# First block's output product as three fp32r products, one eighth of it inside the recurrence

## The chip, the cores and the metric
The kernel runs on one core of a Trainium2 chip. The metric is device time in microseconds, median of three runs. The engines are TensorE (PE, with its weight loads as PEld), VectorE (DVE), ScalarE (ACT), GpSimd (POOL) and SyncE (SP), which issues most loads. All waits between them are semaphores that the kernel sets itself.

## The reference
Two transformer blocks of 256 tokens, width 1024, all in fp32. The change lies in the first one:

```python
x = x + FFN_HALF * swiglu(rms_norm(x, norm_ffn1), ffn1_gate, ffn1_up, ffn1_down)
p = rms_norm(x, norm_mix) @ w_in
o_sb = stick_breaking_attention(q, k, v)      # 8 heads of 64, then rms_norm per head
o_rw = rwkv7_time_mix(rw_in, ...)             # 8 heads of 64, a recurrence in chunks of 64 tokens
x = x + jnp.concatenate([o_sb, o_rw], axis=-1) @ w_out          # 1024 x 1024: the changed product
x = x + FFN_HALF * swiglu(rms_norm(x, norm_ffn2), ffn2_gate, ffn2_up, ffn2_down)

# recurrence: S_t = S_{t-1} diag(w_t) + (S_{t-1} a_t) b_t^T + v_t k_t^T ;  y_t = S_t r_t
# end of rwkv7_time_mix, per head:
yn = (y - mean) * lax.rsqrt(var + LNX_EPS) * ln_w + ln_b
return (yn + bonus) * g
```

## The kernel before
**Data.** Activations between products lie transposed, features on the 128 partitions and 256 tokens along the row. SBUF is cut by hand: `ring` holds six weight slots of 2048 columns, `arena` 27 blocks of 1024 columns (`A(j)`, `tiles(j)`; `AR(j)` is the same memory as fp32r). PSUM is `ps`, eight banks of 512. A weight matrix streams through the ring; the load of item n waits until item n - 6 is used (`w_used`).

**Precision.** Most products are done as three fp32r products (`mm3`, L824): an operand is split into a rounded high part and the rest, and high*high, low*high and high*low are summed. For weights ScalarE makes the high part (L1612) and VectorE subtracts the rest in the ring slot (`split`, L2179). The output product used plain fp32 instead: one `mm` (L774), which the trace shows as two records.

**Order.** Each engine runs its own list; nothing is scheduled at run time. The recurrence is a loop over four chunks. In each, TensorE makes the right side, ScalarE copies it (`rhs_kept`), TensorE multiplies by the inverse (`rec_u`), VectorE copies that (`u_kept`), TensorE adds it to the state and to y, VectorE scales the state (L2478 to L2480), ScalarE copies y (`y_kept`). Beside it VectorE finishes one quarter of the attention half per chunk (`sb_out`, L2464 and L2465). After the last chunk:

1. TensorE takes head means (`y_mean`), VectorE centres y, ScalarE squares it, TensorE takes variances (`y_var`), ScalarE the root (`y_root`), VectorE the reciprocal (L2499), the product (L2500) and the sum (L2501), which is the recurrent half of the mix (`rw_out`).
2. The output product is `out_rows(N_WOUT, c)` for c = 0 to 3: 128 x 512 products, two feature tiles f by two token tiles t by two halves h, so 8 per c and 32 in all, summed in banks 4 to 7. c = 0 and 1 need the attention half, c = 2 and 3 the recurrent half. c = 0 stands in two halves around the variances.
3. Then the next feed-forward begins: ScalarE and VectorE split its first three weight tiles, VectorE adds the product to x (`add_rows`, L2205), ScalarE squares the rows and takes roots, VectorE scales (L2173), TensorE transposes (`turn_apart`, L795).

On VectorE the three splits stand between `rw_out` and `add_rows`:

```python
tt(mix[1], y_n, bonus, ALU.add).then_inc(S("rw_out"), 1)
for n in range(HI_RING):
    split(N_FFN2 + n)
add_rows("x2_done", N_WOUT + 4, 1.0)
norm_rows("n3")
```

## Time and profile before

| | |
|---|---|
| time of three runs | 1105.42 us median (1105.32 to 1107.82) |
| the profiled execution's own time | 1107.49 us |
| its span, first to last instruction | 1105.7 us |
| TensorE busy, weight loads | 98%, 81% |
| VectorE, ScalarE, GpSimd busy | 61%, 41%, 3% |
| chain that ended last | TensorE 89%, VectorE 6%, ScalarE 3% |
| mean granted clock of TensorE | 0.997 of 2.4 GHz; digit 9 in all 40 slices |

The profile gives each instruction's start and length. "Idle before" is the time in which the engine waited, with the instruction that released it. The chain is followed back from the last instruction. Ends of matmuls are modelled and overlap, so the distance of two starts is a better measure of a matmul than its length. "Busy" for TensorE means that some matmul was in flight, not that it ran at its best. All times of the rows are from the span's start; the changed part lies at 340 to 397 us.

### The profile page before, as it was taken

The page shows a single profiled execution, that of the slowest core. Times are in us where ns is not written, and L with a number is a line of the kernel's source. Part 1 is how long each engine was busy: PE and PEld are TensorE (multiplying, and loading weights), DVE is VectorE, ACT ScalarE, POOL GpSimd, SP SyncE. Part 2 cuts the span into 40 slices and gives each one's busy share as a digit, 9 for nine tenths or more (in the row PEclk, how much of TensorE's full clock was granted, in tenths as well). Part 3 has the DMA queues.
Part 4 walks back from the last instruction along what each step waited for, and adds up shares of the span by engine and source line. Part 5 has one row for each costly group of instructions (what it writes and reads, how often), then busy time and mean ns, then how long its engine had stood idle before and what let it go on. Part 6 is the DMA issues. An engine that isn't in the chain of part 4 may idle for free.

```text
span 1105.7 us, 19149 instructions
## 1 busy us (share of the span) xinstructions
PE 1086.0 (98%) x8232; PEld 892.5 (81%) x8232; DVE 672.0 (61%) x848; ACT 448.1 (41%) x573; POOL 35.3 (3%) x30
## 2 busy tenths in 40 slices
PE   9999999999999999999999999999999999999997
PEld 8999999999988479999988999988999753434343
DVE  6488777789564856778766573277559542222123
ACT  6333334764542254333325242467583521211112
POOL 0000000000340000000003000000000000000000
PEclk9999999999999999999999999999999999999999
DMA  9976756454300349689862353332357979999994
GB/s 333 391 264 227 255 183 202 142 155 151 116 3 2 114 158 332 233 287 333 306 218 76 114 193 113 115 115 83 109 195 298 373 316 408 421 410 418 421 419 198
DMA packets 121012, 254.29 MB, mean 230 GB/s; under 512 B 6241, under 2 KB 91505, under 8 KB 109426
## 3 DMA queue, kind: packets, MB, share of 16 engines
q1 hardware_dynamic: 119890, 250.54, 62.1%
q10 hardware_dynamic: 1056, 2.79, 0.8%
q8 instruction: 51, 0.84, 0.3%
q14 instruction: 15, 0.12, 0.0%
HBM read 252.25 MB, written 1.06 MB: 229 GB/s over the span
## 4 chain that ended last, share of the span: by engine, by line
PE 89%; DVE 6%; ACT 3%; issue 1%; DMA 0%; SPq 0%; ACTq 0%; DVEq 0%
PE ps L827 54%; PE ps L774 33%; ACT arena L1612 2%; DVE ring_r L2179 1%; ACT arena_r L1612 1%; DVE ring_r L2312 1%; PE ps L1357 1%; DVE arena L2499 1%; DVE arena L2366 1%; DMA x<-in_x 0%; DVE arena L2381 0%; PE ps L795 0%; ACT gb_r L1612 0%; PE ps L1562 0%; PE ps L783 0%
## 5 line engine op out<-in xcount | busy, mean ns | idle before, releaser
L827 PE MATMUL ps<-hall_r,arena_r 128*128 128x256 f32 x1632 | 299.6, 281 | 0.0
L827 PE MATMUL ps<-arena_r 128*128 128x256 f32 (+1 forms) x1216 | 286.3, 325 | 0.0
L2179 DVE TENSOR_TENSOR ring_r<-ring,arena_r 128x2048 fp32r<-128x2048 f32 x88 | 203.1, 2312 | 109.4 <-ACT arena_r L1612 106.9
L827 PEld LDWEIGHTS ps<-hall_r,arena_r 128*128 128x128 f32 x1632 | 252.8, 188 | 1.2 <-issue 0.3
L1612 ACT ACTIVATE arena_r<-ring 128x2048 fp32r<-128x2048 f32 (+1 forms) x101 | 191.1, 1899 | 150.1 <-PE ps L827 139.8
L827 PE MATMUL ps<-hall_r,ring_r 128*128 128x256 f32 x816 | 227.8, 279 | 0.0
L827 PEld LDWEIGHTS ps<-arena_r 128*128 128x128 f32 x1216 | 203.9, 189 | 18.9 <-issue 0.7
L1612 ACT ACTIVATE arena<-ps 128x512 f32<-128x512 f32 (+3 forms) x136 | 80.4, 605 | 302.2 <-PE ps L827 188.0
L774 PE MATMUL ps<-arena 64*64 64x32 f32 (+7 forms) x1944 | 188.6, 321 | 4.1 <-ACT arena L1612 1.3
L774 PEld LDWEIGHTS ps<-arena 128*64 128x64 f32 (+3 forms) x1944 | 110.7, 143 | 64.8 <-issue 57.0
L827 PEld LDWEIGHTS ps<-hall_r,ring_r 128*128 128x128 f32 x816 | 154.9, 190 | 0.9
L827 PE MATMUL ps<-arena_r,ring_r 128*128 128x256 f32 (+1 forms) x432 | 123.4, 286 | 0.0
L827 PE MATMUL ps<-ring_r,arena_r 128*128 128x512 f32 (+1 forms) x336 | 117.9, 351 | 0.0
L827 PEld LDWEIGHTS ps<-arena_r,ring_r 128*128 128x128 f32 x432 | 82.7, 192 | 0.7
L827 PEld LDWEIGHTS ps<-ring_r,arena_r 128*128 128x128 f32 x336 | 63.1, 188 | 9.2
L774 PE MATMUL ps<-ring,arena 128*64 128x512 f32 (+1 forms) x256 | 70.0, 593 | 0.3 <-issue 0.2
L2829 DVE TENSOR_TENSOR arena<-arena,ps 128x512 f32<-128x512 f32 x8 | 5.5, 688 | 89.6 <-PE ps L774 89.6
L774 PEld LDWEIGHTS ps<-ring,arena 128*64 128x64 f32 (+1 forms) x256 | 26.5, 150 | 41.4 <-issue 40.4
L2223 DVE SCALAR_TENSOR_TENSOR arena<-arena,vec 128x1024 f32<-128x1024 f32 x40 | 50.4, 1280 | 0.3
L1612 ACT ACTIVATE arena_r<-arena 128x512 fp32r<-128x512 f32 (+1 forms) x24 | 17.7, 736 | 62.8 <-DVE arena L2847 60.2
L1612 ACT ACTIVATE arena<-ps,small 128x512 f32<-128x512 f32 (+1 forms) x46 | 27.6, 622 | 26.7 <-PE ps L827 13.2
L2847 DVE SCALAR_TENSOR_TENSOR arena<-ps,arena,gb 128x512 f32<-128x512 f32 x16 | 12.0, 751 | 38.7 <-PE ps L774 22.6
(274 smaller groups left out, 1144.2 us busy)
## 6 DMA issues: line engine op xcount, KB each, us to landing
ring<-in_w_in SPq DMA_DIRECT2D x35, 1024.0 KB, 5.2
arena<-in_w_exp_down SPq DMA_DIRECT2D x32, 1024.0 KB, 11.8
ring<-in_ffn_up SPq DMA_DIRECT2D x22, 1024.0 KB, 5.3
ring<-in_ffn_down SPq DMA_DIRECT2D x22, 1024.0 KB, 4.9
ring<-in_ffn_gate SPq DMA_DIRECT2D x21, 1024.0 KB, 6.5
arena<-in_w_mod SPq DMA_DIRECT2D x18, 1024.0 KB, 9.2
arena<-in_w_exp_up SPq DMA_DIRECT2D x16, 1024.0 KB, 14.5
ring<-in_w_exp_gate SPq DMA_DIRECT2D x16, 1024.0 KB, 11.4
```

Of the source, the lines that this page charges most:

```text
L774: return pe.matmul(out_, lhsT, rhs, start=start, stop=stop, skip_group_check=group)
L827: m = pe.matmul(out_, w[i], h[j], start=start and i + j == 0, stop=stop and j == 1, skip_group_check=group)
L1357: m = pe.transpose(ps[:, 2 + t, k * P:(k + 1) * P], att[h % 2][:, t, k * P:(k + 1) * P], ident)
L1612: return act.activation(out_, in_, func, **kw)
L2179: tt(lo(n), slot(n), hi(n), ALU.subtract).then_inc(S("w_lo"), 1)
L2223: m = stt(acc, w, c_col, acc, ALU.mult, ALU.add)
L2312: tt(lo_cols(n), slot(n).rearrange("p (k n) -> p k n", k=KT), win_hi(j), ALU.subtract).then_inc(S("win_lo_v"), 1)
L2366: link(v.reciprocal(sq, sq))
L2499: link(v.reciprocal(y_n, y_n))
L2829: tt(by_twos(hs, "f p"), by_twos(hs, "f p"), by_twos(ps[:, 1, :], "p f"), ALU.mult).then_inc(S("hs"), 1)
L2847: stt(y_e[:, h, :], ps[:, 2 + h, :], gate_s, gb[:, 1, h * 512:(h + 1) * 512], ALU.mult, ALU.mult).then_inc(S("y_full"), 1)
```

## The change
- The whole output product is done with `mm3`. Its weights' high parts go into four free places (`wo_hi`), copied by ScalarE (`out_weights_high`), one in each chunk of the recurrence; their low parts are subtracted in the ring slots by GpSimd (`wo_lo`).
- The mix is split in eight tiles of 128x256: ScalarE rounds (`mix_high`), VectorE subtracts (`mix_rest`). The attention half moves from block 26 to block 3.
- The end of the recurrent half is done in quarters: reciprocal, product and sum of 128x256 four times, with the split of each quarter behind the sum of the next.
- Four of the 32 triples (c = 0, f = 0) are issued inside the recurrence, two in its third and two in its fourth chunk (`first_out_piece`). The other half of c = 0 stands before the variances.
- The recurrence uses banks 0 to 3: state sums move from bank 7 to 3, and y has bank 2 alone, so it waits for the copy of the chunk before instead of two chunks before.
- One load of the later modulation stream waits for the end of the output product, since its target now holds a high part.

```diff
         z_b = ps[:, 0:2, :].rearrange("p h (k n) -> p h k n", k=4)
-        mix = [tiles(26), tiles(2)]
+        mix = [tiles(3), tiles(2)]
+        mix_hi, mix_lo = ([AR(j).rearrange("p (k n) -> p k n", k=4) for j in blks] for blks in ((5, 4), (3, 2)))
+        wo_hi = [AR(25, SLOT), hall_r[:, 0].rearrange("p k n -> p (k n)"), hall_r[:, 1].rearrange("p k n -> p (k n)"),
+                 gb_r[:, :, :].rearrange("p g n -> p (g n)")]
         inv_t, inv_tt, inv_x = (A(j).rearrange("p (i n) -> p i n", n=CH) for j in (23, 11, 15))
...
                     sp.wait_ge(*W("rec_y", NCH))
+                elif tag == "f2" and i == 2:
+                    sp.wait_ge(*W("w_used", N_WOUT + 4))
                 elif tag == "f2" and i == 3:
...
 
+            for c in range(4):
+                pool.wait_ge(*W("wo_hi", c + 1))
+                pool.tensor_tensor(lo(N_WOUT + c), slot(N_WOUT + c), wo_hi[c], ALU.subtract).then_inc(S("wo_lo"), 1)
+
             pool.wait_ge(*W("mod_kept", 3))
...
 
-            def out_rows(n0, c, fs=range(2)):
-
-                weight(n0 + c)
+            def out_rows(c, fs=range(2)):
+
+                n = N_WOUT + c
+                pe.wait_ge(*W("wo_lo", c + 1))
+                w = [z.rearrange("p (k n) -> p k n", k=2) for z in (wo_hi[c], lo(n))]
                 for f, t, hs_ in last_first(c == 3, fs):
-                    lhs = mix[c // 2][:, 2 * (c % 2) + f, :]
+                    pe.wait_ge(*W("mix_lo", 2 * c + f + 1))
+                    heads_ = [z[c // 2][:, 2 * (c % 2) + f, t * P:(t + 1) * P] for z in (mix_hi, mix_lo)]
                     for h in hs_:
-                        m = mm(ps[:, 4 + 2 * t + h, :], lhs[:, t * P:(t + 1) * P],
-                               rows(n0 + c)[:, f, h * 512:(h + 1) * 512],
-                               start=c == 0 and f == 0, stop=c == 3 and f == 1, group=True)
+                        m = mm3(ps[:, 4 + 2 * t + h, :], heads_, [z[:, f, h * 512:(h + 1) * 512] for z in w],
+                                start=c == 0 and f == 0, stop=c == 3 and f == 1, group=True)
                     if c == 3 and (f, t + h) == (1, 1):
...
                 for h in range(8):
-                    o = ps[(h % 2) * HD:(h % 2 + 1) * HD, 7, (h // 2) * HD:(h // 2 + 1) * HD]
+                    o = ps[(h % 2) * HD:(h % 2 + 1) * HD, 3, (h // 2) * HD:(h // 2 + 1) * HD]
                     mm(o, k_tok[:, c // 2, h * HD:(h + 1) * HD],
...
                 for h in range(8):
-                    o = ps[(h % 2) * HD:(h % 2 + 1) * HD, 7, (h // 2) * HD:(h // 2 + 1) * HD]
+                    o = ps[(h % 2) * HD:(h % 2 + 1) * HD, 3, (h // 2) * HD:(h // 2 + 1) * HD]
                     m = mm(o, b_tok[:, c // 2, h * HD:(h + 1) * HD],
...
             def rec_y_at(c, h):
-                return ps[(h % 2) * HD:(h % 2 + 1) * HD, 2 + c % 2, (h // 2) * CH:(h // 2 + 1) * CH]
+                return ps[(h % 2) * HD:(h % 2 + 1) * HD, 2, (h // 2) * CH:(h // 2 + 1) * CH]
 
             def rec_y_v(c):
-                if c >= 2:
-                    pe.wait_ge(*W("y_kept", c - 1))
+                if c:
+                    pe.wait_ge(*W("y_kept", c))
                 for h in range(8):
...
                 m.then_inc(S("rec_y"), 1)
+
+            def first_out_piece(t, h):
+                pe.wait_ge(*W("wo_lo", 1))
+                pe.wait_ge(*W("mix_lo", 1))
+                w = [z.rearrange("p (k n) -> p k n", k=2) for z in (wo_hi[0], lo(N_WOUT))]
+                mm3(ps[:, 4 + 2 * t + h, :], [z[0][:, 0, t * P:(t + 1) * P] for z in (mix_hi, mix_lo)],
+                    [z[:, 0, h * 512:(h + 1) * 512] for z in w], stop=False, group=True)
 
...
                     rec_state_v(c)
+                if c >= 2:
+                    first_out_piece(c - 2, 0)
                 if c == 0:
...
                     rec_y_v(c)
+                if c >= 2:
+                    first_out_piece(c - 2, 1)
                 pe.wait_ge(*W("u_kept", c + 1))
...
 
-            pe.wait_ge(*W("sb_out", 4))
-            out_rows(N_WOUT, 0, (0,))
+            out_rows(0, (1,))
             pe.wait_ge(*W("y_sq", 2))
             four(2, lambda o, k: mm(o, head_mean, sq[:, k, :]), "y_var")
-            out_rows(N_WOUT, 0, (1,))
-            out_rows(N_WOUT, 1)
-            pe.wait_ge(*W("rw_out", 1))
-            out_rows(N_WOUT, 2)
-            out_rows(N_WOUT, 3)
+            out_rows(1)
+            out_rows(2)
+            out_rows(3)
             pe.wait_ge(*W("y_root", 1))
...
             keep_sums(5)
+
+            def mix_high(k):
+                act.wait_ge(*(W("rw_out", k - 3) if k >= 4 else W("sb_out", k + 1)))
+                f(mix_hi[k // 4][:, k % 4, :], mix[k // 4][:, k % 4, :], ACT.Copy).then_inc(S("mix_hi"), 1)
+
+            def out_weights_high(c):
+                n = N_WOUT + c
+                act.wait_ge(*W(f"w_in_slot{n % RING}", 16 * (n // RING + 1)))
+                f(wo_hi[c], slot(n), ACT.Copy).then_inc(S("wo_hi"), 1)
+
             for c in range(NCH):
...
                     f(kn, banks(4), ACT.Sqrt, bias=EPS_COL).then_inc(S("sbo_root"), 1)
+                else:
+                    mix_high(c - 1)
+                out_weights_high(c)
                 act.wait_ge(*W("rec_y", c + 1))
-                f(y_rw[:, :, c * CH:(c + 1) * CH], ps[:, 2 + c % 2, 0:256].rearrange("p (k n) -> p k n", k=4),
+                f(y_rw[:, :, c * CH:(c + 1) * CH], ps[:, 2, 0:256].rearrange("p (k n) -> p k n", k=4),
                   ACT.Copy).then_inc(S("y_kept"), 1)
+            mix_high(3)
             for j in range(2):
...
             f(y_n, banks(2), ACT.Sqrt, bias=LNX_COL).then_inc(S("y_root"), 1)
+            for k in range(4, 8):
+                mix_high(k)
             for t in range(TT):
...
 
+            def mix_rest(k):
+                v.wait_ge(*W("mix_hi", k + 1))
+                tt(mix_lo[k // 4][:, k % 4, :], mix[k // 4][:, k % 4, :], mix_hi[k // 4][:, k % 4, :],
+                   ALU.subtract).then_inc(S("mix_lo"), 1)
+
             for c in range(NCH):
...
                 v.tensor_copy(u_z[rows_, c % 2, :], ps[rows_, 1, :]).then_inc(S("u_kept"), 1)
+                if c:
+                    mix_rest(c - 1)
                 if c < NCH - 1:
                     v.wait_ge(*W("rec_state", c + 1))
-                    sums = ps[:, 7, 0:256].rearrange("p (k n) -> p k n", k=4)
+                    sums = ps[:, 3, 0:256].rearrange("p (k n) -> p k n", k=4)
                     if c:
...
 
+            mix_rest(3)
             for k in range(4):
...
             v.wait_ge(*W("y_root", 1))
-            link(v.reciprocal(y_n, y_n))
-            link(tt(y_n, y_c, y_n, ALU.mult))
-            tt(mix[1], y_n, bonus, ALU.add).then_inc(S("rw_out"), 1)
+            for k in range(4):
+                link(v.reciprocal(y_n[:, k, :], y_n[:, k, :]))
+                link(tt(y_n[:, k, :], y_c[:, k, :], y_n[:, k, :], ALU.mult))
+                tt(mix[1][:, k, :], y_n[:, k, :], bonus[:, k, :], ALU.add).then_inc(S("rw_out"), 1)
+                if k:
+                    mix_rest(3 + k)
+            mix_rest(7)
             for n in range(HI_RING):
```

TensorE, third chunk of the recurrence, from the right side's state part to the y products. Names in brackets are semaphores; `rhs_kept` is ScalarE's copy, `u_kept` VectorE's. Before:

```order
L774 MATMUL ps<-arena 64x64 [waits state]
L774 MATMUL ps<-arena 64x64 x15
L774 MATMUL ps<-arena 64x64 [waits rhs_kept]
L774 MATMUL ps<-arena 64x64 x7
L774 MATMUL ps<-arena 64x64 [waits y_kept]
L774 MATMUL ps<-arena 64x64 x7
L774 MATMUL ps<-arena 64x64 [waits u_kept]
```

After (`first_out_piece` is the three rows of 128x512, twice):

```order
L783 MATMUL ps<-arena 64x64 [waits state]
L783 MATMUL ps<-arena 64x64 x15
L836 MATMUL ps<-arena_r 128x512 [waits mix_lo,wo_lo]
L836 MATMUL ps<-arena_r 128x512
L836 MATMUL ps<-ring_r,arena_r 128x512
L783 MATMUL ps<-arena 64x64 [waits rhs_kept]
L783 MATMUL ps<-arena 64x64 x7
L783 MATMUL ps<-arena 64x64 [waits y_kept]
L783 MATMUL ps<-arena 64x64 x7
L836 MATMUL ps<-arena_r 128x512 [waits mix_lo,wo_lo]
L836 MATMUL ps<-arena_r 128x512
L836 MATMUL ps<-ring_r,arena_r 128x512
```

Three fp32r products now stand before the wait for ScalarE's copy and three before the wait for VectorE's.

VectorE, from the root (`act_rms`) to the scaling for the next norm; the 128x2048 rows are the weight splits, the rows on x the row additions. Before:

```order
L2499 RECIPROCAL arena<-arena 128x1024 [waits act_rms,v_step]
L2500 TENSOR_TENSOR arena<-arena 128x1024 [waits v_step]
L2501 TENSOR_TENSOR arena<-arena 128x1024 [waits v_step]
L2179 TENSOR_TENSOR ring_r<-ring,arena_r 128x2048 [waits w_hi] x3
L2205 SCALAR_TENSOR_TENSOR x<-ps,x 128x512 [waits row_part] x3
L2205 SCALAR_TENSOR_TENSOR x<-ps,x 128x512 [waits w_used]
L2171 RECIPROCAL small<-small 128x1 [waits each_root]
L2173 TENSOR_SCALAR arena<-x,small 128x1024 [waits v_step]
```

After, from the split of the third quarter on:

```order
L2505 TENSOR_TENSOR arena_r<-arena,arena_r 128x256 [waits mix_hi]
L2543 RECIPROCAL arena<-arena 128x256
L2544 TENSOR_TENSOR arena<-arena 128x256 [waits v_step]
L2545 TENSOR_TENSOR arena<-arena 128x256 [waits v_step]
L2505 TENSOR_TENSOR arena_r<-arena,arena_r 128x256 [waits mix_hi] x2
L2214 TENSOR_TENSOR ring_r<-ring,arena_r 128x2048 [waits w_hi] x3
L2240 SCALAR_TENSOR_TENSOR x<-ps,x 128x512 [waits row_part] x3
L2240 SCALAR_TENSOR_TENSOR x<-ps,x 128x512 [waits w_used]
L2206 RECIPROCAL small<-small 128x1 [waits each_root]
L2208 TENSOR_SCALAR arena<-x,small 128x1024 [waits v_step]
```

The splits still stand behind the mix and ahead of the additions; the mix before them has sixteen instructions in place of three.

ScalarE, from the squares (`dve_out`) to the norm's first square; the DMAs load the context rows, the three copies of 128x2048 are the next weights' high parts. Before:

```order
L1612 ACTIVATE arena<-arena 128x512 [waits dve_out] x2
L1612 ACTIVATE arena<-ps,cst 128x1024 [waits pe_rms]
L1894 DMA arena<-in_ctx 128x1024 x2
L1612 ACTIVATE arena_r<-ring 128x2048 [waits w_in_slot2]
L1612 ACTIVATE arena_r<-ring 128x2048 [waits w_in_slot3]
L1612 ACTIVATE arena_r<-ring 128x2048 [waits w_in_slot4]
L1612 ACTIVATE arena,small<-x 128x1024 [waits x2_done]
```

After:

```order
L1631 ACTIVATE arena<-arena 128x512 [waits dve_out] x2
L1631 ACTIVATE arena<-ps,cst 128x1024 [waits pe_rms]
L1631 ACTIVATE arena_r<-arena 128x256 [waits dve_out] x4
L1929 DMA arena<-in_ctx 128x1024 x2
L1631 ACTIVATE arena_r<-ring 128x2048 [waits w_in_slot2]
L1631 ACTIVATE arena_r<-ring 128x2048 [waits w_in_slot3]
L1631 ACTIVATE arena_r<-ring 128x2048 [waits w_in_slot4]
L1631 ACTIVATE arena,small<-x 128x1024 [waits x2_done]
```

Four roundings of mix quarters, each waiting for VectorE, now stand between the root and the DMAs with the weight copies.

## Rows read from the trace of the kernel before
**Rows 1.** The chain of waits, 325 to 400 us: start us, us, what.
```profile
369.99 6.57 DVE arena L2499
...
379.11 14.01 PE ps L774 x32
...
393.15 0.69 DVE x L2205
```
**Rows 2.** TensorE's timeline: start us, us, engine line op, count [idle before <-releaser].
```profile
351.92 1.61 PE L774 MATMUL ps<-arena 128*64 128x64 f32 x32 [0.21 <-ACT arena L1612]
353.84 3.49 PE L774 MATMUL ps<-arena 128*64 128x64 f32 x80 [0.31 <-DVE arena L2472]
358.01 1.61 PE L774 MATMUL ps<-arena 128*64 128x64 f32 x32 [0.68 <-ACT arena L1612]
...
363.41 3.60 PE L774 MATMUL ps<-ring,arena 128*128 128x512 f32 x8
366.84 1.89 PE L774 MATMUL ps<-arena,cst 128*128 128x256 f32 x8
368.57 24.55 PE L774 MATMUL ps<-ring,arena 128*128 128x512 f32 x56
394.85 1.95 PE L795 MATMUL ps<-cst,arena 128*128 128x128 f32 x16 [1.73 <-DVE arena L2173]
...
421.18 0.64 PE L827 MATMUL ps<-arena_r 128*128 128x512 f32 x2
...
426.75 0.28 PE L827 MATMUL ps<-hall_r,arena_r 128*128 128x256 f32 x1
```
**Rows 3.** VectorE's timeline.
```profile
294.48 1.76 DVE L2407 SCALAR_TENSOR_TENSOR arena<-arena,vec 128x1024 f32<-128x1024 f32 x1
...
354.57 0.42 DVE L2478 TENSOR_TENSOR arena<-ps,arena 128x256 f32<-128x256 f32 x1 [0.79 <-PE ps L774]
355.03 0.42 DVE L2480 TENSOR_TENSOR arena<-arena,small 128x256 f32<-128x256 f32 x1
355.38 1.75 DVE L2464 RECIPROCAL arena<-arena 128x256 f32<-128x256 f32 x1
...
378.98 6.69 DVE L2179 TENSOR_TENSOR ring_r<-ring,arena_r 128x2048 fp32r<-128x2048 f32 x3
389.72 1.29 DVE L2205 SCALAR_TENSOR_TENSOR x<-ps,x 128x512 f32<-128x512 f32 x2 [4.05 <-PE ps L774]
...
394.96 0.16 DVE L2171 RECIPROCAL small<-small 128x1 f32<-128x1 f32 x1 [0.26 <-ACT small L1612]
```
**Rows 4.** ScalarE's timeline; ACTq is its queue that issues DMAs.
```profile
336.61 1.11 ACT L1612 ACTIVATE arena<-ps,cst 128x1024 f32<-128x1024 f32 x1 [0.43 <-PE ps L774]
...
361.14 0.38 ACT L1612 ACTIVATE arena<-ps 128x256 f32<-128x256 f32 x1 [3.18 <-PE ps L774]
...
368.78 0.82 ACTq L1894 DMA_DIRECT2D arena<-in_ctx  x2
369.78 3.70 ACT L1612 ACTIVATE arena_r<-ring 128x2048 fp32r<-128x2048 f32 x2
...
391.04 1.06 ACT L1612 ACTIVATE arena<-x 128x1024 f32<-128x1024 f32 x1 [11.65 <-DVE x L2205]
...
393.88 0.63 ACT L1612 ACTIVATE arena<-x 128x512 f32<-128x512 f32 x1 [0.42 <-DVE x L2205]
```
**Rows 5.** GpSimd's timeline.
```profile
317.63 2.00 POOL L721 TENSOR_TENSOR arena<-arena,cst 128x1024 f32<-128x1024 f32 x1 [4.67 <-PE ps L774]
```
**Rows 6.** The page's groups: xcount | busy us, mean ns | idle before.
```profile
L2223 DVE SCALAR_TENSOR_TENSOR arena<-arena,vec 128x1024 f32<-128x1024 f32 x40 | 50.4, 1280 | 0.3
```
**Rows 7.** TensorE's timeline at the start and near 607 us.
```profile
1.14 6.11 PE L774 MATMUL ps<-c_pad 128*128 128x256 f32 x16 [1.14 <-POOL c_pad L703]
...
607.29 2.08 PE L774 MATMUL ps<-cst,hall 128*64 128x4 f32 x32
```
**Rows 8.** Stretches: from:to us, length, busy of PE, PEld, DVE, ACT, POOL, granted clock, DMA share, GB/s.
```profile
610.40:613.70 3.30, 3.30 (x18) 3.30 (x18) 0.08 (x2) 0.00 (x0) 0.00 (x0) 0.52 0.00 0
```

More of the change, by code:

```diff
@@ L186, in build @@
                          ("gain_kept", 2), ("n6_gained", 3), ("n6_inv", 2)],
-            "dve_out": [("sb_out", 4), ("y_centred", 2), ("rw_out", 1)],
+            "dve_out": [("sb_out", 4), ("y_centred", 2), ("rw_out", 4)],
             "dve_tail": [("lam_prod", 1), ("head_gain", 1), ("y_four", 2), ("y_mix", 4),
```

## The prediction
> **What bounds the kernel now.** I read the page of the profile first: TensorE is busy 98% of a span of 1105.7 us, so time is only won where TensorE works less or waits less, and only if nothing else is then late. The chain of waits around the output product shows who that would be [rows 1]: from 369.99 to 379.1 it runs on VectorE (reciprocal, product and sum that make the recurrent half of the mix), then 14.01 us on TensorE (that half's 16 products), then VectorE's last row addition at 393.15. TensorE's timeline [rows 2] shows the other side: it starts the 28 products after the variances at 368.57 and has no idle row until 394.85. So two paths are even here: VectorE's chain is ready at 379.1, and TensorE has just worked up to it. VectorE's timeline [rows 3] shows its slack after that: three weight splits from 378.98 to 385.67, then 4.05 us of idle before the row additions. ScalarE [rows 4] has more.
>
> **What TensorE gains.** An fp32 product of 128x512 is two records; 56 records in 24.55 us give 0.877 us per product. Three fp32r products of that size: the feed-forward's down product does 8 such triples between 421.18 and 426.75 [rows 2], 0.696 us each. So 32 x (0.877 - 0.696) = 5.8 us less TensorE work, and 4 of the 32 triples (2.8 us) are moved into chunks three and four.
>
> **The recurrence (later by about 1.2 us).** A chunk is a chain TensorE, ScalarE copy, TensorE, VectorE copy. TensorE's idle before the second half of chunk three is 0.21 us (351.92), before its third part 0.31 (353.84), in chunk four 0.68 (358.01) and, in a row alike, 0.32. A triple of 0.696 put into each gap costs the excess: 0.48 + 0.38 + 0.01 + 0.38 = 1.25 us. If weight loads hide 0.14 us more per gap it is 0.8; if nothing is hidden, 2.8. I take 1.25. The bank changes cost nothing: y is copied out at the head of ScalarE's free time over 3 us before the next y is written, and state starts after the same wait on the copy of banks 2 and 3. What must be ready: the weights' high parts, one ScalarE copy of 1.85 us per chunk, fit between the rhs copy and the y copy (at least 3.2 us idle there; in chunk one they follow the root that ends at 337.7) [rows 4]; their low parts on GpSimd, 128x2048, have no row, the nearest is 2.00 us for 128x1024 [rows 5], so 4 us each. The first is there by about 344, wanted at 352; the last by 366, wanted at 382. VectorE's added subtraction of 0.42 us falls into its 0.79 us wait for the state [rows 3].
> A GpSimd subtraction lies beside VectorE's work from 361 to 365. A VectorE instruction of 128x1024 took 1.76 us at 294.48, when GpSimd began to work, against 1.28 on the mean of 40 of its form [rows 3, 6], so this could cost VectorE up to 0.5 us before the root (GpSimd only adds work, so it gains nothing); I take 0, since about 0.4 us of slack stands there.
> The Trainium skill (GPSIMD Engine Reference, its table of specifications) says that GpSimd shares its SBUF interfaces with VectorE and contends with instructions that have two SBUF inputs; the 1.76 us agrees. By that rule the sum would be 0.1 to 0.5 us higher.
>
> **Up to the root (later by 0.6 us).** Means, then the second half of product 0 as four triples: 2.78 us instead of 3.43 (363.41 to 366.84). The variances start 1.25 - 0.65 = 0.6 later, and the root ends at 370.5 instead of 369.9.
>
> **VectorE's chain, where the step is decided.** Before: 9.1 us from 369.99 to the mix, splits to 385.67, that is 15.7 us. After, by quarters: reciprocal 1.75 (the row of 128x256; four are 7.0 against 6.57 for one of 128x1024), product 0.42 + 0.04, sum with 0.35 to the next start [rows 3]: 2.6 us each, and a subtraction of 0.38 in two of them before the last sum: 11.2 us to the last sum. Then ScalarE rounds that quarter (0.38). Behind it in ScalarE's order now stand the two context DMAs (0.82 us to issue, hidden under the root before [rows 4]) and the three weight copies, which before ran from 369.78, under the reciprocal. Now the first copy starts at 12.05 and ends at 13.95; VectorE's three splits (6.69) end at 20.7 after the root, at 370.57 + 20.7 = 391.3 instead of 385.67. They stand ahead of the row additions in VectorE's order.
> TensorE: product 1 ends near 374.7; quarter five is ready at about 376.2, six at 379.1, seven and eight at 382.1 and 382.6. So it ends at 382.1 + 8 x 0.696 = 387.7, 5.4 us earlier than 393.1, and finds nothing to do: its results wait 3.6 us for VectorE.
> Four additions at 0.645 [rows 3] end at 393.9, as before (393.84). What is worse: before, the norm's ScalarE work on the first rows ran from 391.04, under TensorE's last products. Now those rows are added only at 392.6. The square takes 1.06, its read and root some 0.45 (from 393.88 + 0.63 to 394.96), so the first root is there at 394.1, 0.26 behind the last addition; before, the first transpose came 1.0 behind that addition, now about 1.35: 395.2 instead of 394.85. The second rows take two more such steps of 1.0 to 1.05: root at 396.1 instead of 394.93 [rows 3, 4], last transpose ended about 1.05 later than before: **+1.05 us** with the clock unchanged. The next feed-forward is TensorE without an idle row, so the shift stays.
>
> **The clock.** TensorE now does nothing from 387.7 to 395.2, 7.5 us. Before, nothing like this occurs near: the longest idle time here is 1.73 us [rows 2], and the page's clock row keeps its highest digit. But elsewhere, after 2.08 us with only 128x4 products (607.29), the granted clock was 0.52 from 610.40 to 613.70, that is 1.2 GHz, and then 2.4 again under full work [rows 7, 8]. And the run's own start: the first 16 records of 128x256 take 6.11 us, where the eight variance records take 1.89 and eight more would take 1.73. The 2.5 us too much are 5.0 us at half speed by an estimate, though the granted clock doesn't show it. So I expect 1.2 GHz when the transposes begin, for 3.3 to 5.0 us of work bound by TensorE, half of it lost, with the 0.7 us of waiting for the second rows absorbed: 0.35 + 1.65 = +2.0 to 0.35 + 2.5 = +2.85. **I take +2.4 us.**
> The Trainium skill (TensorE: Matmul & The Clock Gate, Part 1) says that idleness throttles the array to 1.2 GHz and sustained activity releases it; of the two cases, +1.05 and +2.4, the rule gives the second, and row 607.29 agrees with it.
>
> **Sum.** The profiled execution took 1107.49 us (span 1105.7 and 1.8 around it), 2.1 above the median 1105.42; two of the three runs stand at the median. Its own time would become 1109.9, the median 1107.8.
>
> **Rivals.**
> (A) TensorE's gain arrives: -5.4 us, 1100.0. It holds if the end is set by TensorE, so if splits or the quartered chain overlap where I have them in line. For it: TensorE's 14.01 us on the chain. Against: the splits are three instructions ahead of the additions in one queue, with 4.05 us of slack, and they start 5.6 us later. To end earlier than before at all, VectorE would have to shed over 1 us between the root and the additions.
> (B) Slower beyond noise: the clock stays at 1.2 GHz through the transposes and most of the first gate product, decided when the low stretch outlasts 5.9 us of work. Twice the row's stretch, 6.6 us, gives 0.35 + 3.3 = +3.65, with 0.5 of GpSimd contention +4.15: 1109.6. For it: transposes and waits give a weak start after 7.5 us of nothing. Against: both rows end earlier, at 3.3 and 5.0.
> (C) The clock isn't lowered, or is back before the transposes: +1.05, 1106.5. For it: no fall beside the waits of 1.7 us. Against: this gap is four times as long.
> (D) The moved pieces stall the recurrence: low weights late on GpSimd. At double its rate of the row, 8 us a piece one behind the other, the first is still there at 348 and the last at 372, ten before its use. That costs nothing, so (D) is only a tail of (B).
>
> **Chances.** Forecast (+1.5 to +3.3) 0.50; C 0.19; B 0.22; A with its halves 0.09. What a measurement of this kernel can tell from no change is 0.3%, 3.3 us. Of A some 0.07 lies beyond it; forecast and C within, with a rest of A and B: same 0.72; slower 0.21. The likeliest one's own range is 1106.9 to 1108.7. For 8 in 10 I take C from its lower end and B whole, and an execution like the profiled one: 1105.0 to 1110.4.
>
> **What the profile after will show.** Right: three splits on VectorE that end near 391 with no idle time before the row additions; TensorE idle over 6 us before the transposes; a granted clock near 0.5 just behind them; the root 0.5 to 1 us later; products in triples of 0.70 us; ScalarE's weight copies behind the last rounding. Wrong: TensorE's last product directly followed by its addition (A), the chunks of the recurrence over 2 us longer (my gap sums), or a granted clock of 1.00 from 388 to 400 (C).

## The result and the profile after

| | before | changed | ratio, 95% interval |
|---|---|---|---|
| median, us | 1106.04 (1105.32 to 1107.82, 4 runs) | 1114.57 (1114.38 to 1115.62, 4 runs) | 1.0077 (1.0059 to 1.0094) |
| profiled execution, us | 1107.49, span 1105.7 | 1114.61, span 1112.8 | |

The change makes the kernel slower by 0.8%, 8.5 us. I had said +2.4 us, so the forecast and its range (to 1110.4) are both wrong. The first thing to read is VectorE's timeline through the recurrence and up to the root, against [rows 3]: start us, us, engine line op, count [idle before <-releaser].

```profile
348.26 0.42 DVE L2520 TENSOR_TENSOR arena<-ps,arena 128x256 f32<-128x256 f32 x1 [0.33 <-PE ps L783]
348.72 3.95 DVE L2522 TENSOR_TENSOR arena<-arena,small 128x256 f32<-128x256 f32 x1
352.59 1.74 DVE L2499 RECIPROCAL arena<-arena 128x256 f32<-128x256 f32 x1
...
358.43 3.58 DVE L2505 TENSOR_TENSOR arena_r<-arena,arena_r 128x256 fp32r<-128x256 f32 x1
361.93 0.41 DVE L2520 TENSOR_TENSOR arena<-ps,arena 128x256 f32<-128x256 f32 x1
...
367.06 1.75 DVE L2499 RECIPROCAL arena<-arena 128x256 f32<-128x256 f32 x1
368.84 3.29 DVE L2500 SCALAR_TENSOR_TENSOR arena<-arena,vec 128x256 f32<-128x256 f32 x1
372.17 1.28 DVE L2528 TENSOR_TENSOR arena<-arena,ps 128x512 f32<-128x512 f32 x2
...
377.85 1.75 DVE L2543 RECIPROCAL arena<-arena 128x256 f32<-128x256 f32 x1
...
391.78 6.70 DVE L2214 TENSOR_TENSOR ring_r<-ring,arena_r 128x2048 fp32r<-128x2048 f32 x3 [1.94 <-ACT arena_r L1631]
```

Three instructions of 128x256, which take 0.42 to 0.48 us elsewhere, take 3.95, 3.58 and 3.29. GpSimd's timeline of the same kernel says what stands beside them:

```profile
339.37 4.54 POOL L759 TENSOR_TENSOR ring_r<-ring,arena_r 128x2048 fp32r<-128x2048 f32 x1 [14.02 <-ACT arena_r L1631]
347.87 4.52 POOL L759 TENSOR_TENSOR ring_r<-ring,hall_r 128x2048 fp32r<-128x2048 f32 x1 [3.96 <-ACT hall_r L1631]
357.18 4.54 POOL L759 TENSOR_TENSOR ring_r<-ring,hall_r 128x2048 fp32r<-128x2048 f32 x1 [4.79 <-ACT hall_r L1631]
367.31 4.54 POOL L759 TENSOR_TENSOR ring_r<-ring,gb_r 128x2048 fp32r<-128x2048 f32 x1 [5.59 <-ACT gb_r L1631]
```

The last three end at 352.39, 361.72 and 371.85; VectorE's long rows end at 352.67, 362.01 and 372.13, each 0.28 or 0.29 later. What VectorE did meanwhile with PSUM as one of its two inputs (348.26) or with one input (the reciprocal, 367.06) kept its time. This looks like a wait for GpSimd's whole instruction, not like a slower rate.

TensorE's timeline, against [rows 2]:

```profile
352.72 1.62 PE L783 MATMUL ps<-arena 128*64 128x64 f32 x32 [2.65 <-DVE arena L2522]
354.28 1.22 PE L836 MATMUL ps<-arena_r 128*128 128x512 f32 x2
...
355.85 2.39 PE L783 MATMUL ps<-arena 128*64 128x64 f32 x32
...
383.58 0.70 PE L836 MATMUL ps<-hall_r,arena_r 128*128 128x512 f32 x2 [1.84 <-DVE arena_r L2505]
...
402.32 3.43 PE L804 MATMUL ps<-cst,arena 128*128 128x128 f32 x16 [5.84 <-DVE arena L2208]
405.51 0.48 PE L783 MATMUL ps<-hall_r,arena_r 128*128 128x256 f32 x2
```

Stretches of the changed kernel, columns as in [rows 8] (the granted clock is the third number from the right):

```profile
354.28:358.10 3.82, 3.82 (x36) 3.08 (x35) 0.82 (x3) 2.44 (x3) 0.92 (x1) 0.57 0.00 0
...
385.14:388.45 3.31, 3.31 (x9) 2.60 (x8) 3.24 (x5) 0.42 (x1) 0.00 (x0) 0.52 0.38 129
...
402.30:405.20 2.90, 2.88 (x14) 2.90 (x15) 1.23 (x4) 1.43 (x5) 0.00 (x0) 0.50 0.00 0
610.40:613.70 3.30, 3.30 (x31) 3.30 (x30) 2.02 (x1) 0.60 (x1) 0.00 (x0) 1.00 0.02 5
```

The 2.65 us wait at 350.1 is followed by 1.56 us of small products at nearly full clock and then, from 354.28, by a stretch mostly at 1.2 GHz (mean 0.57), in which 32 small products take 2.39 us instead of 1.61. Behind the 1.84 us wait at 381.7 the clock falls too, from 385.14 to 388.45. The wait before the transposes is followed by a third such stretch, and the 16 transposes take 3.43 us instead of 1.95.

The stage's account, from these rows and those of before: the first reciprocal behind the root comes at 377.85 instead of 369.99, **+7.86**. From there to the first transpose it is 24.47 us instead of 24.86 (394.85 - 369.99), -0.39. From the first transpose to the first gate product it is 3.19 us; before it was 1.84 (396.69 - 394.85), +1.35. Sum +8.82. Nothing is gained or lost after that up to the 32 small products of 128x4: they start at 616.12 instead of 607.29 [rows 7], 8.83 later. The spans differ by only 7.1, because the low stretch of before at 610 us, about 1.6 us of lost work [rows 8], isn't there in this profile.

### The profile page after: what moved, and what is told of

Same layout as the page of the kernel before. It is cut to its first block, busy times and chain, and to the rows that moved or that the text cites. A ratio compares the mean times of both kernels' runs of the same rounds, so it can differ in the third digit from the quotient of the medians.

```text
span 1112.8 us, 19252 instructions
## 1 busy us (share of the span) xinstructions
PE 1084.4 (97%) x8264; PEld 899.9 (81%) x8264; DVE 685.3 (62%) x865; ACT 458.6 (41%) x585; POOL 53.4 (5%) x34
## 4 chain that ended last, share of the span: by engine, by line
PE 84%; DVE 8%; ACT 4%; DMA 3%; issue 1%; SPq 0%; ACTq 0%; DVEq 0%
PE ps L836 54%; PE ps L783 28%; DMA arena<-in_w_exp_up 2%; ACT arena L1631 1%; DVE ring_r L2214 1%; ACT arena_r L1631 1%; DVE ring_r L2347 1%; DVE arena L2543 1%; PE ps L1376 1%; DVE arena L2401 1%; PE ps L804 1%; DVE arena_r L2505 0%; DMA x<-in_x 0%; DVE arena L2416 0%; DVE arena L2522 0%
## 5 line engine op out<-in xcount | busy, mean ns | idle before, releaser
L836 PE MATMUL ps<-hall_r,arena_r 128*128 128x256 f32 (+1 forms) x1664 | 311.1, 284 | 1.8 <-DVE arena_r L2505 1.8
L836 PE MATMUL ps<-arena_r 128*128 128x256 f32 (+1 forms) x1232 | 290.6, 325 | 0.0
L836 PEld LDWEIGHTS ps<-hall_r,arena_r 128*128 128x128 f32 x1664 | 259.5, 188 | 5.0 <-issue 2.6
L836 PE MATMUL ps<-ring_r,arena_r 128*128 128x512 f32 (+1 forms) x368 | 131.3, 357 | 0.0
L836 PEld LDWEIGHTS ps<-ring_r,arena_r 128*128 128x128 f32 x368 | 69.6, 189 | 10.8
L1631 ACT ACTIVATE arena_r<-arena 128x512 fp32r<-128x512 f32 (+2 forms) x32 | 21.0, 657 | 77.3 <-DVE arena L2894 60.2
L783 PE MATMUL ps<-ring,arena 128*64 128x512 f32 x192 | 41.9, 592 | 0.2 <-issue 0.2
L783 PEld LDWEIGHTS ps<-ring,arena 128*64 128x64 f32 x192 | 14.4, 137 | 26.6 <-issue 26.6
```

The costliest lines, as they stand in the source:

```text
L783: return pe.matmul(out_, lhsT, rhs, start=start, stop=stop, skip_group_check=group)
L836: m = pe.matmul(out_, w[i], h[j], start=start and i + j == 0, stop=stop and j == 1, skip_group_check=group)
L1631: return act.activation(out_, in_, func, **kw)
```

## The experiments

Three readings of the long rows stood against each other. **H**, hold: VectorE's instruction with two SBUF inputs waits until GpSimd's instruction has ended. **S**, shared rate: both engines slow each other by the amount of data. **B**: the new banks or the fp32r pieces delay the recurrence. Beside them **P** (the price of the pieces), **K** (the clock after the gap) and **Q** (the order of VectorE's queue behind the root) were to be sized.

**1. Each GpSimd subtraction in eight pieces**, the same data:

```
for g in range(8):
    cut = slice(256 * g, 256 * g + 256)
    m = pool.tensor_tensor(lo(...)[:, cut], slot(...)[:, cut], wo_hi[c][:, cut], ALU.subtract)
```

> The changed kernel with each GpSimd subtraction of 128x2048 cut into eight of 128x256 (same data, same waits). Theory H (hold): a VectorE instruction with two SBUF tensor inputs that meets a running GpSimd subtraction ends only when that GpSimd instruction has ended, so the three long rows (3.95, 3.58, 3.29 us in place of 0.42, 0.42, 0.48) become at most 1.0 us each; the root comes 5 to 6 us earlier than in the changed kernel, time about 1109 (1108 to 1110.5). Rival S (shared rate: both engines are slowed while they overlap, whatever the lengths): the same total overlap, so the rows keep most of their excess, 1113 to 1115. Rival B (the recurrence waits because y and state have fewer banks): unchanged, 1114.6.

Measured 1108.58 us, ratio 1.0018 (1.0008 to 1.0028), so 6 us of the 8.5 are gone. VectorE's timeline (the same instruction as at 348.72), then GpSimd's:

```profile
348.97 0.84 DVE L2526 TENSOR_TENSOR arena<-arena,small 128x256 f32<-128x256 f32 x1
...
356.19 0.83 DVE L2526 TENSOR_TENSOR arena<-arena,small 128x256 f32<-128x256 f32 x1
```
```profile
348.11 5.92 POOL L761 TENSOR_TENSOR ring_r<-ring,hall_r 128x256 fp32r<-128x256 f32 x8 [2.97 <-ACT hall_r L1635]
```

The wait falls from 3.5 us to 0.4 although GpSimd is busy longer with the same bytes. S falls; the length of one GpSimd instruction counts. The root comes at 371.48, 6.37 us earlier than in the changed kernel, a little more than expected.

**2. GpSimd's work before the recurrence.** ScalarE's high parts are made at 310 to 317 and at 334, GpSimd's low parts at 320 to 340.5:

```
-            for c in range(4):
-                pool.wait_ge(*W("wo_hi", c + 1))
+            for i, c in enumerate((1, 2, 3, 0)):
+                ...
+                pool.wait_ge(*W("wo_hi", i + 1))
```

> The changed kernel with the output weights' high parts copied by ScalarE before the recurrence (three in its idle time at 310 to 317 us, the fourth at 334) and GpSimd's four subtractions of 128x2048 behind them (about 320 to 340 us), where VectorE's instructions have at most one SBUF tensor input. H: no long VectorE row is left in the recurrence, the root comes 0.6 to 1.0 us later than in the kernel before instead of 7.4 us, time 1.0 to 2.8 us over the kernel before (my prediction's sum, 1107 to 1109). S: the same, since nothing overlaps. B: the recurrence stays long, 1114.6.

Measured 1108.62 us, ratio 1.0022 (1.0012 to 1.0032): **+2.4 us, the size of my forecast**. VectorE's timeline:

```profile
348.84 0.43 DVE L2524 TENSOR_TENSOR arena<-arena,small 128x256 f32<-128x256 f32 x1
...
371.00 1.75 DVE L2545 RECIPROCAL arena<-arena 128x256 f32<-128x256 f32 x1 [0.69 <-ACT arena L1631]
...
384.94 6.69 DVE L2216 TENSOR_TENSOR ring_r<-ring,arena_r 128x2048 fp32r<-128x2048 f32 x3 [1.95 <-ACT arena_r L1631]
```

The same instruction takes 0.43, and the root (the first reciprocal behind it) is 6.85 us earlier than in the changed kernel. With the starts of the same instructions in both kernels one sees where those go: 3.41 in the first held instruction (the next reciprocal at 352.59 instead of 349.18), 0.80 up to VectorE's next copy of u, in the stretch at half clock, 2.11 in the second held one, -0.67 up to the last copy of u, 2.05 up to the bonus additions with the third, -0.85 up to the root. This run also moves ScalarE's copies of the weights; experiments 1 and 3 leave those where they were, so the case against GpSimd doesn't hang on this run alone. TensorE's timeline of this kernel, for P and K:

```profile
351.52 0.74 PE L836 MATMUL ps<-arena_r 128*128 128x512 f32 x2
352.10 0.40 PE L836 MATMUL ps<-ring_r,arena_r 128*128 128x512 f32 x1
352.43 1.61 PE L783 MATMUL ps<-arena 128*64 128x64 f32 x32
...
395.48 3.65 PE L804 MATMUL ps<-cst,arena 128*128 128x128 f32 x16 [7.10 <-DVE arena L2210]
...
399.72 0.64 PE L783 MATMUL ps<-hall_r,arena_r 128*128 128x256 f32 x4
```

**3. The kernel before with GpSimd's instructions alone**: four subtractions of constants, 128x2048, into memory that nothing reads, one per chunk. Nothing else is changed.

```
+            for c in range(NCH):
+                pool.wait_ge(*W("u_kept", c + 1))
+                ...
+                pool.tensor_tensor(unused, cst[:, 0:SLOT], cst[:, 512:512 + SLOT], ALU.subtract)
```

> The kernel before, and nothing of the change but four GpSimd subtractions of 128x2048 on constants, one in each chunk, started when VectorE has copied that chunk's u; their result is used by nothing. H: in chunks two and three the state's scaling (two SBUF inputs) waits about 3.3 us for GpSimd's end, in chunk four the attention quarter's last instruction about 1 us: the root 7 to 8 us later, time 1113 to 1114.5. S: each of these instructions at most doubled, under 1 us each: 1106.5 to 1108.5. B: nothing, since the banks are those of before: 1106.

Measured 1116.5 us, ratio 1.0080 (1.0061 to 1.0100). VectorE's timeline:

```profile
344.95 1.98 DVE L2472 SCALAR_TENSOR_TENSOR arena<-arena,vec 128x256 f32<-128x256 f32 x1
...
348.92 3.64 DVE L2487 TENSOR_TENSOR arena<-arena,small 128x256 f32<-128x256 f32 x1
...
357.55 3.64 DVE L2487 TENSOR_TENSOR arena<-arena,small 128x256 f32<-128x256 f32 x1
```

And one row of TensorE's:

```profile
363.08 4.73 PE L780 MATMUL ps<-arena 128*64 128x64 f32 x64 [0.68 <-ACT arena L1618]
```

The old product in the old banks is as slow as the changed kernel once GpSimd has four such instructions. B falls, and H is shown from the other side. Four VectorE rows are long here, and each ends 0.27 to 0.29 us behind GpSimd's end. The time is above the expected 1113 to 1114.5: the root comes at 378.78, 8.79 us later than before instead of the expected 7 to 8, because behind the second of two waits of 2.34 us TensorE's granted clock is 0.50 from 363 to 372 us (the row above: 64 small products in 4.73 us; the 32 of 358.01 [rows 2] take 1.61). That the total equals the whole change's is chance: here all 8.8 us arise before the root, in the changed kernel 7.9 do and the clock behind the gap adds the rest.

**4. GpSimd copies in place of the subtractions**, one input and less than half the time. The low parts are then the whole weights, so this kernel leaves out the subtraction and its result is another one; only its times are used:

```
-  pool.tensor_tensor(lo(N_WOUT + c), slot(N_WOUT + c), wo_hi[c], ALU.subtract)
+  pool.tensor_copy(lo(N_WOUT + c), slot(N_WOUT + c))
```

> The changed kernel with GpSimd's four subtractions replaced by copies with one input (the low parts of the output weights are then the whole weights, so that part of the result is another one). H in its wide form (any GpSimd instruction on SBUF holds VectorE's two-input ones): the long rows end with the copies; if a copy takes 2 us, as twice a memset of 128x1024 does (0.95 us), each row has about 0.5 to 1.5 us too much and the time is 1108.5 to 1111. H in its narrow form (only GpSimd instructions with two SBUF inputs hold): no long rows, 1107 to 1109. B: 1114.6.

Measured 1109.02 us, ratio 1.0026 (1.0015 to 1.0037). VectorE's row, then GpSimd's:

```profile
348.89 1.29 DVE L2522 TENSOR_TENSOR arena<-arena,small 128x256 f32<-128x256 f32 x1
```
```profile
348.01 1.90 POOL L759 CAST ring_r<-ring 128x2048 fp32r<-128x2048 f32 x1 [6.61 <-ACT hall_r L1631]
```

VectorE's row ends at 350.18, 0.27 behind GpSimd's end at 349.91. So GpSimd needs only one input from SBUF to hold VectorE, and the price again goes with how much of its instruction is still to run.

**5. TensorE kept busy in the gap**: experiment 2 with 14 products of zeros, 128x256, into a free bank behind the output product.

```
+            for i in range(14):
+                mm(ps[:, 0, 0:256], zeros[:, 0:P], zeros)
```

> The kernel with early GpSimd work (e2_early) and 14 products of zeros, 128x256, on TensorE after the output product, into a bank that nothing uses, about 6.0 of its 7.1 us of idle time. Theory K (the clock's fall costs as my prediction had it): the granted clock stays 1.00, the transposes start at the same time (395.5) and take about 2.6 us instead of 3.65, the first gate product runs at full speed from the start: 1.2 to 1.8 us faster than e2_early, so +0.6 to +1.2 us against the kernel before. Rival N (the slow stretch is hidden behind the waits for ScalarE and VectorE): no change against e2_early, +2.4 us.

Measured 1108.72 us, ratio 1.0015 (1.0006 to 1.0024), against 1.0022 in experiment 2: -0.8 us with overlapping intervals, less than the 1.2 to 1.8 expected. The trace is sharper. TensorE's timeline, and below it one stretch of this kernel:

```profile
388.27 6.21 PE L783 MATMUL ps<-c_pad 128*128 128x256 f32 x28
395.44 1.09 PE L804 MATMUL ps<-cst,arena 128*128 128x128 f32 x8 [0.96 <-DVE arena L2212]
397.05 1.09 PE L804 MATMUL ps<-cst,arena 128*128 128x128 f32 x8 [0.52 <-DVE arena L2212]
398.04 0.47 PE L783 MATMUL ps<-hall_r,arena_r 128*128 128x256 f32 x2
```
```profile
395.50:399.00 3.50, 2.98 (x24) 2.65 (x25) 2.12 (x6) 2.33 (x8) 0.00 (x0) 1.00 0.00 0
```

The same stretch of experiment 2:

```profile
395.50:399.00 3.50, 3.50 (x17) 3.50 (x18) 1.87 (x6) 2.02 (x7) 0.00 (x0) 0.50 0.00 0
```

At full clock the first gate product starts at 398.04 instead of 398.78, and the fifth product at 398.58 instead of 399.72. The clock costs 1.14 us here; my term was 1.35 (2.4 - 1.05).

**6. Another order behind the root**: experiment 2 with ScalarE's next-weight copies between the roundings of the mix, and only the first of VectorE's three splits ahead of the row additions, the others in later gaps.

```
-            for n in range(HI_RING):
-                split(N_FFN2 + n)
+            split(N_FFN2)           # the other two after the norm's rows and the context rows
```

> e2_early with another order behind the recurrence: ScalarE makes the next weights' three high parts between the roundings of the mix quarters, and VectorE does only the first of the three splits ahead of the row additions, the second behind the norm's columns, the third behind the context rows. Theory Q (TensorE's 5.4 us are real and are held back only by VectorE's queue): row additions follow TensorE, the transposes start near 390 instead of 395.5, TensorE idles under 2.5 us before them and the clock stays up; of some 6.5 to 7 us against e2_early about 1 us is given back at the context transposes or the up product: 1101 to 1102.5, -4 to -5.5 us against the kernel before. Rival: the splits behind the norm hold up the next products by as much as they free, within 1 us of e2_early.

Measured 1102.53 us, ratio 0.9965 (0.9953 to 0.9977), at the edge of the expected 1101 to 1102.5. TensorE's timeline:

```profile
390.11 2.06 PE L804 MATMUL ps<-cst,arena 128*128 128x128 f32 x16 [1.74 <-DVE arena L2210]
392.06 0.47 PE L783 MATMUL ps<-hall_r,arena_r 128*128 128x256 f32 x2
```

The gap of 7.1 us is down to 1.74, the transposes run at full clock, and the first gate product starts 6.72 us earlier than in experiment 2. So the gain of the shorter product was there; the order behind the root had kept it. ScalarE's copies and two of VectorE's three splits were moved together, and no run separates the two.

**7. No pieces in the recurrence**: experiment 2 with the four triples back between the means and the variances, all in one change of TensorE's order.

```
-                if c >= 2:
-                    first_out_piece(c - 2, 0)
```

> e2_early without products inside the recurrence: the four triples stand between the means and the variances, the other four of product 0 behind the variances. Theory P (pieces inside the chain cost what exceeds its gaps, 1.25 us by my sum, and buy nothing, since VectorE sets the end): root 1.1 to 1.4 us earlier, time 1.0 to 1.5 us less than e2_early, about +1.0 to +1.4 against the kernel before. Rival: the variances wait for nothing else and TensorE sets the end, so the 2.8 us come back behind the recurrence: the same or 1 us slower.

Measured 1108.03 us, ratio 1.0011 (1.0002 to 1.0021). TensorE's timeline, then VectorE's:

```profile
351.69 1.61 PE L783 MATMUL ps<-arena 128*64 128x64 f32 x32 [0.21 <-ACT arena L1628]
353.61 3.49 PE L783 MATMUL ps<-arena 128*64 128x64 f32 x80 [0.31 <-DVE arena L2511]
357.78 1.61 PE L783 MATMUL ps<-arena 128*64 128x64 f32 x32 [0.68 <-ACT arena L1628]
```
```profile
369.11 1.75 DVE L2542 RECIPROCAL arena<-arena 128x256 f32<-128x256 f32 x1 [0.69 <-ACT arena L1628]
```

The gaps are those of [rows 2] again, to the hundredth, though y and state now live in banks 2 and 3: the bank changes cost nothing. The root comes 1.89 us earlier than with the pieces, more than the 1.1 to 1.4 expected. By the ratios (1.0011 against 1.0022, overlapping intervals) 1.2 us are left: without the pieces the low stretch behind the gap reaches further into the gate products, of which four take 1.05 us at 397.88 instead of 0.64 at 399.72.

**8. Both** (6 and 7 together):

> e6_order and e7_no_pieces together. If both theories hold and VectorE's quarters still set TensorE's last products: 0.5 to 1.2 us faster than e6_order, 1100 to 1101.5. If TensorE sets the end once the order is mended, the 2.8 us moved out of the recurrence come back in part: up to 1.5 us slower than e6_order.

Measured 1101.27 us, ratio 0.9955 (0.9942 to 0.9969): faster than the kernel before and the lowest of all, though its interval overlaps that of experiment 6. TensorE's timeline:

```profile
389.12 2.06 PE L804 MATMUL ps<-cst,arena 128*128 128x128 f32 x16 [1.73 <-DVE arena L2207]
391.07 0.47 PE L783 MATMUL ps<-hall_r,arena_r 128*128 128x256 f32 x2
```

The first gate product starts 5.62 us earlier than before (396.69), close to the 5.8 that the product saves.

**All runs at one mark.** The start of TensorE's 32 small products of 128x4 (607.29 before) lies ahead of the low stretch near 610 us that some profiles have and others don't. It agrees with the ratios within 0.8 us:

| kernel | start, us | against before | ratio as us (of 1106) |
|---|---|---|---|
| before | 607.29 | | |
| changed | 616.12 | +8.83 | +8.5 |
| 1, GpSimd in pieces | 610.11 | +2.82 | +2.0 |
| 2, GpSimd early | 609.79 | +2.50 | +2.4 |
| 3, before with GpSimd's four | 616.07 | +8.78 | +8.8 |
| 4, GpSimd copies | 610.83 | +3.54 | +2.9 |
| 5, TensorE kept busy | 608.63 | +1.34 | +1.7 |
| 6, other order | 603.35 | -3.94 | -3.9 |
| 7, no pieces | 608.43 | +1.14 | +1.2 |
| 8, both | 602.39 | -4.90 | -5.0 |

## Why the prediction was wrong

- **The step that failed: "this could cost VectorE up to 0.5 us before the root ...; I take 0"**, and with it rival D, which says "That costs nothing" of longer GpSimd instructions. The step cost 6.85 us at the root (changed kernel against experiment 2), some 6.1 by the ratios (1.0077 - 1.0022). I asked only when GpSimd's results would be ready, looked at one of its four subtractions (361 to 365) for what it does to VectorE, and read 1.76 instead of 1.28 as a rate. It was the end of a wait. GpSimd's timeline of the kernel before, beside the 294.48 of [rows 3], would have told, and so would a second place, at 308 us:

```profile
294.07 1.09 POOL L733 TENSOR_TENSOR arena<-arena,cst 128x512 f32<-128x512 f32 x1
295.12 2.07 POOL L730 TENSOR_TENSOR arena<-arena,cst 128x512 f32<-128x512 f32 x1
...
308.55 4.41 POOL L721 TENSOR_TENSOR arena<-arena,cst 128x1024 f32<-128x1024 f32 x2
```
```profile
308.70 2.41 DVE L2415 TENSOR_TENSOR arena<-arena,cst 128x512 f32<-128x512 f32 x1
```

  VectorE's instruction (294.48 to 296.24) ends 1.08 us after GpSimd's end at 295.16, nearly its own 1.28 from there. GpSimd's next one then takes 2.07 instead of 1.09 and ends at 297.19, 0.95 after VectorE's end. Two rows in turn, each with a wait for the other's end. At 308.70 VectorE takes 2.41 for 128x512, where such rows take 0.69 elsewhere: it starts just behind GpSimd's first instruction of 128x1024 (2.00 us by its like) and ends 0.6 behind that one's end; the second takes 2.46. With a wait for the whole instruction, a 4-us GpSimd instruction beside a VectorE chain on the path costs the chain up to 4 us, and three of four do so here, by 3.52, 3.17 and 2.81 us on the held rows.
  The Trainium skill (SBUF — State Buffer, "Who interferes with whom") calls the pair of ports that the two engines share an exclusive lock: a VectorE instruction with two SBUF inputs contends with a GpSimd instruction that reads SBUF, and one with at most one SBUF input, outside the 2-port modes, doesn't. By that rule the rows at 348.26 and 367.06 are untouched and those at 348.72, 358.43 and 368.84 wait; the trace agrees in all five. That the wait lasts for the whole instruction the section says of VectorE's 2-port modes; for two SBUF inputs it is what the ends of the rows here show. The prediction had weighed only the "contention" of the Trainium skill (GPSIMD Engine Reference, its table of specifications), which left the size open.
- **A consequence that I hadn't priced**: the hold makes TensorE wait 2.65 us, and a stretch at 1.2 GHz follows, 0.80 us more by the starts above.
- **The pieces**: forecast 1.25, measured 1.76: from the products behind the second chunk's copy of u to the first mean it is 15.58 us in experiment 2 (347.65 to 363.23) and 13.82 in experiment 7 (347.53 to 361.35) and before. A triple between small fp32 products occupies 0.90 us (351.52 to 352.43, and so four times, 3.59 in all), not 0.696. The 0.696 came from a row of triples one behind the other. With the gaps' idle time of 1.52 that would give 2.07, 0.31 too much; the ends of matmuls are modelled, so the distance of starts is the better measure. The range of 0.8 to 2.8 held.
- **Up to the root**: forecast +0.6, measured +1.01 (371.00 against 369.99). The excess is the pieces' 0.5; the shorter second half of product 0 gives 0.64 back (means to variances 4.62 instead of 5.26), as forecast (0.65), and the stretch starts 0.12 earlier.
- **VectorE's chain and the splits**: right. From root to first transpose I had 24.6 us (395.2 - 370.57); experiment 2 has 24.48, the changed kernel 24.47. The splits run without a gap up to the additions (384.94 and 6.69 us of work, with additions from 391.55), TensorE idles 7.1 us in experiment 2 (forecast 7.5).
- **The clock**: right in kind and near in size. 1.2 GHz when the transposes begin, 1.14 us lost against 1.35. In the changed kernel the idle time was 5.84, since TensorE had its own stretch of 3.3 us at half clock at 385.14 and ended later.
- **Banks, ScalarE's copies, DMAs**: right at nothing (experiment 7's gaps; copies of 1.90 us in ScalarE's idle time; experiment 2 is 2.49 us behind at the fifth gate product, 399.72 against 397.23, and 2.50 at the mark, so no later load cost anything).
- **Rival A** (TensorE's gain arrives, 1100.0): not in this change, but by moving two splits and the copies, experiments 6 and 8, 1102.53 and 1101.27. Its condition was named rightly.

So the sum without GpSimd gave 1107.8, and the kernel without GpSimd's work in the recurrence took +2.4 us; one term at zero made the forecast wrong by 6. That experiment 2 meets +2.4 so closely is in part luck: its first transpose came 0.63 us later than before instead of 0.35, and less was lost behind it than forecast, 1.9 against 2.05.

**Open:** why the low stretch at 610 us appears in some profiles (before, experiments 3, 4, 5 and 7) and not in others (changed kernel, experiments 1, 2, 6 and 8). It moves a single span by some 1.6 us, so the ratios, and not spans, carry the verdicts. That VectorE and GpSimd exclude each other through their access to SBUF is the account of the Trainium skill (the section named above); the runs show the waits and which operands have them.

## What to carry to other kernels

Work put on an idle engine is priced by what it does to its neighbours: before a long GpSimd instruction is laid beside a VectorE chain on the path, take its whole length as VectorE's possible wait, cut it into pieces (experiment 1) or put it where VectorE has slack (experiment 2). If one row of a shape is longer than its mean, look whether it ends when the neighbour's instruction ends: a wait scales with the neighbour's length, a rate with one's own. And if a bound engine becomes faster, look at once at what is queued ahead of its consumer: two of three splits and ScalarE's copies, moved, turned +2.4 us into -3.9.

## What the hardware showed that I had not expected

- VectorE with two SBUF inputs waits for the end of GpSimd's instruction, subtraction or copy, and ends 0.27 to 0.29 us behind it for 128x256; with PSUM as one input, or with one input, it doesn't wait.
- GpSimd took 4.54 us for a subtraction of 128x2048 into fp32r, 2.00 for 128x1024 into fp32 [rows 5] (no run separates the width from the type), and 5.5 to 6.2 for eight of 128x256, some of it spent beside VectorE's rows; a copy of 128x2048 takes 1.90.
- Three fp32r products of 128x512 occupy 0.90 us between small fp32 products, 0.696 among their like.
- The granted clock fell behind short waits: 2.65 us inside the recurrence, whose products are small (mean 0.57 from 354.28 to 358.10), and 1.84 us among the products of 128x512 (0.52 from 385.14 to 388.45), each time after 1.56 us more of work. Behind 1.73 us ([rows 2], experiment 8) it did not, nor behind the first of the two waits of 2.34 us in experiment 3, though it did behind the second. These rows give no length of wait from which it falls.
